# A fused five-mixer transformer kernel: four places in TensorE's program written in another order, and three spare products

## What is computed

```python
# gated delta rule: sums of squares of q and k for l2norm
q = l2norm(q) * (GDN_DK ** -0.5); k = l2norm(k)
...
# swiglu of the first layer, and behind it the S5 mixer, whose tables depend on parameters alone
x = layer_norm(ALPHA * x + (silu(x @ w1) * (x @ w3)) @ w2, g, b)
u = x @ s5_w_in
b_bar = ((a_bar - 1.0) / lam)[..., None] * (b_re + 1j * b_im)
...
# attention of the second block: 8 heads of 64, 256 queries, 256 keys
s = q_row @ k_band * scale + bias
p = softmax(s)
o = p @ v_band
x = x + concatenate([a, b]) @ w_out
```

## Time and profile before

| | us |
|---|---|
| median of 3 runs | 1369.63 |
| lowest, highest | 1367.96, 1371.76 |
| the profiled execution | 1372.04 |
| its span in the trace | 1370.2 |
| PE busy | 1316.9 (96%) |
| DVE busy | 406.2 (30%) |
| ACT busy | 219.2 (16%) |
| POOL busy | 171.8 (13%) |

### The profile page before, as it was taken

How to read it: one execution, slowest core, us unless ns; L and a number is a source line. 1 busy time by engine, 2 the same in 40 slices (tenths; PEclk the granted TensorE clock), 3 DMA queues, 4 the chain that set the end, 5 groups by cost and what they waited for, 6 DMA issues and landing times.

```text
span 1370.2 us, 23628 instructions
## 1 busy us (share of the span) xinstructions
PE 1316.9 (96%) x10463; PEld 946.1 (69%) x10463; DVE 406.2 (30%) x866; ACT 219.2 (16%) x432; POOL 171.8 (13%) x132
## 2 busy tenths in 40 slices
PE   7998999999999989899999999999989889999997
PEld 6887986877676757546677777777647548666763
DVE  0636544243354345523111110111250431000001
ACT  1452232130111111502001000010020111000000
POOL 1020000407566300000200000000142000000000
PEclk9999999999999999999999999999999999999999
DMA  9424010799252186646999999999993601351610
GB/s 340 148 96 154 1 63 0 175 376 305 95 188 96 66 199 83 223 192 276 347 418 415 409 407 411 419 413 411 361 293 128 245 1 62 123 184 67 240 62 31
DMA packets 96931, 291.96 MB, mean 213 GB/s; under 512 B 5916, under 2 KB 43264, under 8 KB 84576
## 3 DMA queue, kind: packets, MB, share of 16 engines
q1 hardware_dynamic: 82288, 260.46, 52.0%
q0 software_dynamic: 4800, 14.67, 3.6%
q10 hardware_dynamic: 9776, 15.86, 3.5%
HBM read 274.19 MB, written 16.78 MB: 212 GB/s over the span
## 4 chain that ended last, share of the span: by engine, by line
PE 91%; DVE 5%; ACT 2%; issue 1%; DMA 0%; POOL 0%; DVEq 0%; ACTq 0%; POOLq 0%
PE bank L1643 25%; PE bank L2135 17%; PE bank L2152 8%; PE bank L2289 8%; PE bank L1656 6%; PE bank L1947 5%; PE bank L2075 4%; PE bank L1615 3%; PE bank L1649 3%; PE bank L2001 2%; PE bank L1775 1%; PE bank L1789 1%; PE bank L2024 1%; PE bank L1963 1%; PE bank L1829 1%
## 5 line engine op out<-in xcount | busy, mean ns | idle before, releaser
L1643 PE MATMUL bank<-xT,arena 128*128 128x256 f32 x1696 | 377.4, 382 | 2.2 <-ACT arena L1375 1.3
L1643 PEld LDWEIGHTS bank<-xT,arena 128*128 128x128 f32 x1696 | 322.5, 192 | 53.7 <-issue 8.1
L2135 PE MATMUL bank<-arena 128*32 128x352 f32 x3072 | 230.9, 461 | 1.3 <-DVE arena L1139 0.7
L2135 PEld LDWEIGHTS bank<-arena 128*32 128x32 f32 x3072 | 150.3, 110 | 78.6 <-issue 6.5
L2152 PE MATMUL bank<-arena 128*32 128x256 f32 x2112 | 115.9, 379 | 0.0
L2289 PE MATMUL bank<-arena 128*128 128x512 f32 x256 | 111.0, 592 | 0.0
L2152 PEld LDWEIGHTS bank<-arena 128*32 128x32 f32 x2112 | 99.7, 110 | 15.2
L2289 PEld LDWEIGHTS bank<-arena 128*128 128x128 f32 x256 | 48.6, 190 | 58.2 <-issue 57.9
L1184 DVE TENSOR_TENSOR arena<-arena,bank 128x352 f32<-128x352 f32 x24 | 19.2, 801 | 205.2 <-PE bank L2135 205.2
L1304 DVE TENSOR_TENSOR arena<-arena 128x256 f32<-128x256 f32 x32 | 13.6, 425 | 174.7 <-ACT arena L1599 174.7
L1947 PE MATMUL bank<-arena 128*128 128x512 f32 x144 | 63.6, 594 | 0.0
(11 more groups left out here) (368 smaller groups left out, 1257.1 us busy)
## 6 DMA issues: line engine op xcount, KB each, us to landing
arena<-moe_w SPq DMA_DIRECT2D x64, 1408.0 KB, 14.5
arena<-moe_w SPq DMA_DIRECT2D x24, 1536.0 KB, 16.4
arena<-ffn_w SPq DMA_DIRECT2D x33, 1024.0 KB, 10.3
arena<-gdn_w_in SPq DMA_DIRECT2D x8, 2048.0 KB, 10.9
arena<-w_up SPq DMA_DIRECT2D x8, 2048.0 KB, 9.1
arena<-w_down SPq DMA_DIRECT2D x8, 2048.0 KB, 7.8
slot_rows<-arena ACTq DMA_DIRECT2D x1, 9600.0 KB, 47.1
arena<-s_w_glu SPq DMA_DIRECT2D x4, 2048.0 KB, 11.5
```

What stands on the lines that cost most here:

```text
L1643: last = mm(bank[:, at:at + SEQ], w[:, k, P * m:P * m + P], x[:, k, :], start=(k == 0), stop=(k == KT - 1))
L2135: last = mm(banks[i][32 * q:32 * q + 32, 0:EW1], xg[:, t, EK * s + kk], w[:, kk, EW1 * q:EW1 * q + EW1], start=(s == 0 and kk == 0), stop= ...
```

## The change

Square sums go from before tile 22 to before tile 23. Turns 1, 2 and 3 and kernels 1 and 2 of the S5 tables go one tile on; the V tables stay. Three products with the identity are added ahead of the last turn of tokens. In attention the second half of scores(hp + 1) goes behind the transposes of hp, and the transposes are split by token half, each with a wait of its own. The tuples at the top are read by PE, VectorE and ScalarE alike, so takes, skip blocks and stores move with them.

```diff
-S5_TURN_AT = (9, 12, 15, 18)
-S5_KERNEL_AT = (11, 14, 17)
+S5_TURN_AT = (9, 13, 16, 19)
+S5_KERNEL_AT = (11, 15, 18)
...
-                if m == 22:
+                if m == 23:
                     for n in range(NT):
                         square_sums(n)
+                if m == 22:
                     key_product(1)
                 in_product(m)
...
                 s5_kernel(NPIECE - 1, i)
+            pe.wait_ge(norm_v, 3)
+            keep_warm(banks[0], 3)
             turn_x(xres, 1, 2, (banks[4], banks[5]))
...
-            def scores(hp):
-                for n in range(NT):
+            def scores(hp, halves=(0, 1)):
+                for n in halves:
...
                 if hp < 3:
-                    scores(hp + 1)
-                pe.wait_ge(pn_ready, 2 * hp + 2)
-                for kt in range(2):
-                    if hp:
-                        pe.wait_ge(pt_read, 2 * (hp - 1) + kt + 1)
-                    for n in range(NT):
+                    scores(hp + 1, (0,))
+                if hp:
+                    pe.wait_ge(pt_read, 2 * hp)
+                for n in range(NT):
+                    pe.wait_ge(pn_ready, 2 * hp + n + 1)
+                    for kt in range(2):
                         for e in range(2):
                             last = transpose(banks[4 + kt][:, SEQ * e + P * n:SEQ * e + P * n + P], prob[hp % 2][:, n, e, P * kt:P * kt + P])
-                    last.then_inc(pt_done, 1)
+                        if n:
+                            last.then_inc(pt_done, 1)
+                if hp < 3:
+                    scores(hp + 1, (1,))
                 pe.wait_ge(pt_read, 2 * hp + 2)
```

## The result

The changed kernel takes **1362.08 us** (median of 5, 1360.16 to 1364.88); the kernel before, on the same chip, 1369.65 (median of 5). The ratio is 0.9946, 95% interval 0.9932 to 0.9960: 7.4 us or 0.5% less, between 5.5 and 9.3 us. The forecast was 1363.0. The profiled execution of the changed kernel took 1362.20 with a span of 1360.4; that of the kernel before had a span of 1370.2. The two spans differ by 9.8 us, more than the medians.

The account below looks back on a forecast made before the run. The chain is 91% TensorE's own work, so time lies only in PE's idle and low clock. Terms -4.7 - 3.0 + 0.4 = -7.3 from the 1369.63 median, 0.7 given back: 1363.0, range 1359.5 to 1367.6.

Parts of the forecast that it names:

- 0.7 for the median: Whole kernel: a tenth of the sum given back, as the median's runs may have fewer clock falls to win from.
- Square sums, 0: Delta rule: sums a tile later still end 4.7 us ahead of the roots; 0, bounds -0.2 to +0.2.
- Tables, -4.7: Swiglu: turns and kernels a tile later remove turn 2's stall and low clock; -4.7 us, bounds -2.5 to -4.9.
- The cover at turn 3: Swiglu, after tile 18's w3 products (E): VectorE's take done at E + 3.5, PE there at E + 4.2.
- Spare products, -3.0: Last turn of tokens: three products fill the 3.18 us wait and keep the clock up; -3.0 us, bounds -0.2 to -3.3.
- Attention, +0.4: Attention: hides 0.94 us idle but waits 1.45 before the last four transposes; round 6.8 against 6.66; bounds -1.9 to +1.5.
- the term for the last four transposes: Attention round: 0.47 us of transposes, within the sum 1.7 + 1.92 + 0.47 + 1.7 + 1.0 = 6.8.
- The clock at the end of attention, counted as staying, ±1.7: Last values and output product: low clock, priced at 2.8 us, stays; may move by 1.7 either way.
- both rivals that paid with the clock: Attention: clock falls twice, total -3.3, 1366.3 (chance 0.13); or stays low through most of it, slower, 1376.9 (0.04).
- The stall did not move to turn 3: Swiglu rival: turn 2's stall returns whole at turn 3, 1367.0; one case of one gain missing, together 0.15.
- I am wrong if the clock falls in new places: Whole kernel, sign of error: the granted clock falling in new places in the profile after; no size given.
- the rival in attention: Attention: 1.45 us idles among transposes, three times, make the clock fall; two falls +4, total -3.3, 1366.3; chance 0.13.

Follow-up runs that it names:

- the roots': Changed kernel with VectorE's division first and the output product early, plus ScalarE's roots moved from behind tile 23 to behind tile 22: 1346.21 us, ratio 0.9842.

## Why the prediction was right, point by point

The sum was -7.3, less 0.7 for the median: 1363.0. The time was 1362.1. With the sizes that the traces gave the three terms (-4.7, -2.2, +0.75) the sum is -6.2, inside the 5.5 to 9.3 that was measured. That the number came so close is in part luck: one term was too large and one too small, and in the pair of profiles two changes of the clock that stand in no term (-2.8 and +1.7) and 0.9 us behind the last VectorE instruction came on top.

- **Square sums, 0.** Right: the wait is 3.43 us in both, and key_product(2) follows the first key product by 26.48 us before and 26.49 after. The reason given (tile 23 ends when it did) is the one that counts; a tile further it no longer holds, and there the sums are worth -1.5.
- **Tables, -4.7.** Right: -4.72 in the trace, -4.71 with this part alone, -5.1 in its median. The cover at turn 3 was as worked out (E + 3.4 and E + 4.1 against E + 3.5 and E + 4.2). The clock at 415 us stayed up, as counted.
- **Spare products, -3.0.** The mechanism is right (0.40 us of idle where 0.6 was said, six records in 2.84 us, clock up), and in the pair of profiles it is -2.88. Over four traces without them it is -2.2. The term was taken from one execution with 7 us of low clock, which was at the high end. The 0.7 given back for the median, a tenth of all terms, happens to be the size of this one's miss.
- **Attention, +0.4.** Mis-sized: +0.75 with the clock up. The wait is 1.41 us where 1.45 was worked out, and the path of 3.61 us from the scores to PE's transposes is there (1089.98 to 1093.58). What failed is the term for the last four transposes: 0.47 was taken, and standing behind a wait they last 0.59 until the scores start (1093.58 to 1094.17). That makes a round 6.90 instead of 6.8, three times.
- **The clock at the end of attention, counted as staying, ±1.7.** It went, and gave 2.8 us between the first scores and the MLP, more than the 1.7 allowed; a new fall at 1007 us took 1.7 back. The fall at 1007 doesn't belong to the change: it is in eight of the twelve traces, tables alone, spare products alone and attention alone among them, and not in that of the changed kernel with attention as before. Whether the 2.8 us belong to it is open: the fall was in every trace without the edit of the tables and in one of the nine with it.
- **Rivals.** No fall of the clock in attention ahead of the last values, in any trace, so both rivals that paid with the clock are out. The stall did not move to turn 3. "I am wrong if the clock falls in new places" was put too strictly: it did at 1007, and this is no sign of the change.
- The Trainium skill ("TensorE: Matmul & The Clock Gate", "What's actually happening") was cited for the spare products: activity holds the clock up. The runs agree where 3.18 us of idle were filled (51.51 us and the clock at 1.00 in eight traces) and where 3.43 us were taken away (1.00 from 118 to 124 us).
- The Trainium skill's section "A second HAM failure mode: psum-queue depth-cycling" on the same page ("TensorE: Matmul & The Clock Gate") was cited for the rival in attention: small idles between groups of products, repeated, make the clock swing. In the four traces with three idles of 1.41 us among short groups the clock did not swing.

What stays open: why the clock falls at the end of attention in one execution and not in another, whether the edit of the tables changes how often it does, and what the 0.9 us at the very end are. No run has the square sums' move alone, or the roots' without the attention edits; both are read from traces of kernels with other edits in them.

## What to carry to other kernels

When an engine's wait is moved and not removed, follow the waited-for engine's own order: PE's new order was worth nothing until VectorE divided before it took the next maxima, and the two together were worth 3.3 us. A stall that is followed by a low clock costs more than its own length: idles of 2.47 and 0.48 us in the swiglu cost 4.7. And price a fall of the clock from several traces, since one execution shows only one draw.

## What the hardware showed that I had not expected

The same instructions get the low clock in one execution and not in another. Up to 360 us, the kernel before and the one with the tables alone are the same program. Their windows at 28 us, first of before, then of tables alone, and there at 185 us as well (before had 0.50 in that one, shown above):

```profile
28.00:36.00 8.00, 8.00 (x54) 7.48 (x53) 0.59 (x4) 3.42 (x8) 0.00 (x0) 1.00 1.04 367
```

```profile
28.00:36.00 8.00, 8.00 (x34) 7.01 (x34) 2.16 (x10) 4.10 (x7) 0.00 (x0) 0.60 1.05 387
...
184.80:188.00 3.20, 3.20 (x26) 3.04 (x25) 1.98 (x8) 1.11 (x5) 0.00 (x0) 1.00 0.82 329
```

The low clock was at 28 to 36 us in one and not in the other, and the reverse at 185. The same program took 364.29 us up to kernel 0 in one and 362.22 in the other. And the granted clock doesn't tell all: between 12 and 17 us it reads 1.00 both in the kernel before and in the changed kernel with attention as before, yet a record of the same products (L1643, 256 columns) lasted 634 ns in the first and 379 in the second. Thirty runs of the kernel before, on one chip, lay between 1363.32 us (mean granted clock 0.988) and 1374.41 us (0.983), a spread larger than the whole change; each time it was measured, the median of that kernel lay between 1367.7 and 1369.7.
